# Two transformer blocks: where the feed-forward weights' high and low halves are kept

## What is computed

```python
def conv_ffn(x, ffn_w_in, ffn_conv_w, ffn_conv_b, ffn_w_out):      # first block, both layers
    u, gt = jnp.split(x @ ffn_w_in, 2, axis=-1)
    a = dwconv(gt, ffn_conv_w) + ffn_conv_b
    return (jax.nn.silu(a) * u) @ ffn_w_out

def swiglu(t, w_gate, w_up, w_down):                               # second block
    return (jax.nn.silu(t @ w_gate) * (t @ w_up)) @ w_down
...
        if l % 2 == 0:
            ff = swiglu(h, ffn_w_gate[i], ffn_w_up[i], ffn_w_down[i])
        else:
            ff = moe_swiglu(h, router_w[i], moe_w_gate[i], moe_w_up[i], moe_w_down[i])
```

## Time and profile before

| what | value |
|---|---|
| runs | 2827.49, 2829.64, 2831.5 us; median 2829.64 us |
| profiled execution, span from first to last instruction | 2826.4 us |
| TensorE busy | 2735.9 us (97%) |
| VectorE, ScalarE busy | 2110.1 us (75%), 1694.8 us (60%) |
| DMA | 679.10 MB, mean 240 GB/s |
| the first convolutional layer | 425.17 to 625.43 us |
| the second | 1034.95 to 1237.19 us |
| the gated layer | 1394.49 to 1650.80 us |

### The profile page before, as it was taken

How to read it: one execution, slowest core, us unless ns; L and a number is a source line. 1 busy time by engine, 2 the same in 40 slices (tenths; PEclk the granted TensorE clock), 3 DMA queues, 4 the chain that set the end, 5 groups by cost and what they waited for, 6 DMA issues and landing times.

```text
span 2826.4 us, 42789 instructions
## 1 busy us (share of the span) xinstructions
PE 2735.9 (97%) x18410; PEld 2510.4 (89%) x18418; DVE 2110.1 (75%) x2088; ACT 1694.8 (60%) x1856; POOL 71.6 (3%) x114
## 2 busy tenths in 40 slices
PE   7999999999999999989999999999999999999998
PEld 6999989998999989989899999888888888888886
DVE  5777647876767657777567766688888989888896
ACT  4555446554555546645477753577777767676675
POOL 1000000001000000000010000000000000000000
PEclk9999999999999999999999999999999999999999
DMA  7545447745536467624588732598988989898894
GB/s 235 174 140 168 161 164 254 253 135 154 158 126 200 143 208 249 221 64 150 194 293 291 259 99 90 208 382 334 381 340 337 376 346 371 329 387 340 346 368 183
DMA packets 304404, 679.10 MB, mean 240 GB/s; under 512 B 16560, under 2 KB 238032, under 8 KB 261072
## 3 DMA queue, kind: packets, MB, share of 16 engines
q1 hardware_dynamic: 288832, 617.53, 60.8%
q0 software_dynamic: 15376, 58.75, 6.4%
HBM read 675.19 MB, written 4.69 MB: 241 GB/s over the span
## 4 chain that ended last, share of the span: by engine, by line
PE 74%; DVE 15%; ACT 7%; issue 2%; DMA 1%; SPq 0%; ACTq 0%; DVEq 0%
PE bank L571 71%; DVE w_lo L1366 4%; DVE ew_lo L1875 4%; ACT w_hi L1990 3%; DVE ring_tail L1325 1%; PE bank L1172 1%; ACT ring_tail L2059 1%; DMA ring_head<-in_w_in 1%; DVE ring_tail L1327 1%; PE bank L651 1%; DVE std L1301 1%; PE bank L611 1%; DVE gates L1379 1%; DVE ring_low L1288 0%; PE bank L690 0%
## 5 line engine op out<-in xcount | busy, mean ns | idle before, releaser
L1875 DVE TENSOR_TENSOR ew_lo<-ring_head,ew_hi 128x2048 fp32r<-128x2048 f32 x336 | 759.4, 2288 | 41.4 <-ACT ew_hi L2353 41.4
L2353 ACT CAST ew_hi<-ring_head 128x2048 fp32r<-128x2048 f32 x336 | 640.1, 1914 | 224.5 <-PE bank L571 224.4
L571 PE MATMUL bank<-xs_hi,ring_low 128*128 128x256 f32 (+1 forms) x2608 | 510.9, 283 | 0.0
L571 PEld LDWEIGHTS bank<-xs_hi,ring_low 128*128 128x128 f32 (+1 forms) x2608 | 413.4, 189 | 1.5 <-issue 0.7
L571 PE MATMUL bank<-ew_hi,xe_hi 128*128 128x512 f32 x896 | 353.5, 395 | 0.0
L571 PE MATMUL bank<-ew_hi,xe_lo 128*128 128x512 f32 x896 | 349.4, 390 | 0.0
L571 PE MATMUL bank<-ew_lo,xe_hi 128*128 128x512 f32 x896 | 348.8, 389 | 0.0
L571 PE MATMUL bank<-x_hi,w_hi 128*128 128x256 f32 x1152 | 326.3, 291 | 22.5 <-DVE w_lo L1366 14.7
L1366 DVE TENSOR_TENSOR w_lo<-ring_head,w_hi 128x2048 fp32r<-128x2048 f32 x108 | 247.5, 2292 | 130.5 <-ACT w_hi L1990 130.4
L571 PE MATMUL bank<-x_hi,w_lo 128*128 128x256 f32 x1152 | 319.0, 283 | 0.0
L571 PE MATMUL bank<-x_lo,w_hi 128*128 128x256 f32 x1152 | 318.7, 283 | 0.0
(11 more groups left out here) (425 smaller groups left out, 5483.1 us busy)
## 6 DMA issues: line engine op xcount, KB each, us to landing
ring_head<-in_moe_w_gate SPq DMA_DIRECT2D x112, 1024.0 KB, 7.3
ring_head<-in_moe_w_up SPq DMA_DIRECT2D x112, 1024.0 KB, 7.1
ring_head<-in_moe_w_down SPq DMA_DIRECT2D x112, 1024.0 KB, 7.1
ring_head<-in_w_in SPq DMA_DIRECT2D x82, 1024.0 KB, 5.4
ring_tail<-in_ada_w POOLq DMA_DIRECT2D x48, 1024.0 KB, 7.4
ring_head<-in_ffn_w_in SPq DMA_DIRECT2D x44, 1024.0 KB, 6.1
ring_head<-in_ffn_w_out SPq DMA_DIRECT2D x22, 1024.0 KB, 8.2
ring_head<-in_xa_kv SPq DMA_DIRECT2D x16, 1024.0 KB, 5.4
```

The lines of the kernel that those rows point to most:

```text
L571: ins = nc.tensor.matmul(out, lhsT, rhs, start=start, stop=stop, **kw)
L1875: v.tensor_tensor(ew_lo[:, h, :], ring(c % 6), ew_hi[:, h, :].bitcast(F32), ALU.subtract).then_inc(w_used[c % 6], 1)
L2353: a.copy(ew_hi[:, (e * len(PARTS) + c) % DEPTH_HI, :], ring(c % 6)).then_inc(f.count(part_hi), 1)
```

## The change

The high half gets four buffers in place of two, in the bytes that `w_lo` held. The low half is written in place, into `ring_low[s]`. So the slot is TensorE's until it has gone through the chunk: it gives the slot back (`spent`, the increment of `w_used` rides on the next product), and it counts on `ffn_done` that it has used the high half for the last time, on the product before the chunk's last one. ScalarE waits for `ffn_done` of the chunk four before. Ready chunks are counted over all three layers by `ffn_hi` and `ffn_lo`, in place of one count per buffer or slot. The last chunk's low half goes into a high buffer instead; the next stage writes to that ring slot. The first chunk of a layer has its last two low products behind all others. The silu of the gated layer now waits itself for the gate's bank; ScalarE's product high half waits for the down chunk two steps before; two waits of the next stage count one down further. Apart from that, one load of the second block's mixer takes 32 columns in place of 16.

```diff
-                w_hi, w_lo = (in_scope(ffns, n, 2, CH, dt=F32R) for n in ("w_hi", "w_lo"))
+                w_hi = in_scope(ffns, "w_hi", DEPTH_HI, CH, dt=F32R)
...
-        hi_ready = [sem(f"hi_ready{h}") for h in range(2)]
+        ffn_hi, ffn_lo, ffn_done = sem("ffn_hi"), sem("ffn_lo"), sem("ffn_done")
...
-        cuts = [[(c, CW)] for c in (2064, 2320, 2576)] + [[(1536, 16), (2832, 8)]] + ...
+        cuts = [[(c, CW)] for c in (2064, 2320, 2576)] + [[(1536, 32), (2832, 8)]] + ...
...
+        ffn_base = (0, 3 * (FF1 // CW), 6 * (FF1 // CW))
+        def ffn_slot(i, n):
+            if i == 3 * n - 1:
+                return 3 * ((n - 1) % 2) + 2
+            return (0, 1)[i] if i < 2 else (3, 4, 2, 0, 1, 5)[(i - 2) % 6]
+        def ffn_low(i, n):
+            return w_hi[:, (i + 1) % DEPTH_HI, :] if i == 3 * n - 1 else ring_low[:, ffn_slot(i, n), :]
...
             # TensorE
-                def halves(s, k, n):
-                    h = seq[0] % 2
-                    seq[0] += 1
-                    pe.wait_ge(w_used[s], f.next(w_used[s]))
-                    return [tiles(t[:, h, 0:k * n], k) for t in (w_hi, w_lo)]
+                def halves(k):
+                    i = at[0]
+                    at[0] += 1
+                    pe.wait_ge(ffn_lo, ffn_base[which] + (2 if (which, i) == (2, 0) else i + 1))
+                    return i, tiles(w_hi[:, i % DEPTH_HI, :], k), tiles(ffn_low(i, n), k)
+                def released(out, lhsT, rhs, **kw):
+                    nc.tensor.matmul(out, lhsT, rhs, start=False, stop=False, skip_group_check=True).then_inc(ffn_done, 1)
...
-                                mm(out, hi[:, t, cols], x_lo[:, t, :], False, False)
-                                mm(out, lo[:, t, cols], x_hi[:, t, :], False, t == KD - 1, full if (j, t) == (1, KD - 1) else None)
+                                (released if last else mm)(out, hi[:, t, cols], x_lo[:, t, :], start=False, stop=False)
+                                mm(out, lo[:, t, cols], x_hi[:, t, :], False, t == KD - 1, full if last else None)
+                        spent.append(ffn_slot(i, n))
...
             # VectorE
-            def split_low(s, h, last=None):
-                dve.wait_ge(hi_ready[h], f.next(hi_ready[h]))
-                v.tensor_tensor(w_lo[:, h, :], ring(s), w_hi[:, h, :].bitcast(F32), ALU.subtract).then_inc(w_used[s], 1)
+            def split_low(which, i, n, order=None):
+                dve.wait_ge(ffn_hi, ffn_base[which] + (i if order is None else order) + 1)
+                if i == 3 * n - 1:
+                    dve.wait_ge(ffn_done, ffn_base[which] + i + 2 - DEPTH_HI)
+                v.tensor_tensor(ffn_low(i, n), ring(ffn_slot(i, n)), w_hi[:, i % DEPTH_HI, :].bitcast(F32), ALU.subtract).then_inc(ffn_lo, 1)
...
             # ScalarE
-            def split_high(s, h):
+            def split_high(which, i, n):
+                s = ffn_slot(i, n)
                 eng.wait_ge(ffn_loaded[s], f.next(ffn_loaded[s], 16))
-                a.copy(w_hi[:, h, :], ring(s)).then_inc(f.count(hi_ready[h]), 1)
+                if i >= DEPTH_HI:
+                    eng.wait_ge(ffn_done, ffn_base[which] + i + 1 - DEPTH_HI)
+                a.copy(w_hi[:, i % DEPTH_HI, :], ring(s)).then_inc(ffn_hi, 1)
```

More of the change, by code:

```diff
@@ L369, in due, with ffn_steps @@
             return d * folds // span if 0 < d <= span else folds if d > span else 0
-        def ffn_steps(up, down, n, engine, per, f):
+        ffn_base = (0, 3 * (FF1 // CW), 6 * (FF1 // CW))
+        def ffn_steps(up, down, n):
             up(0, 0)
[L374 to L382, removed]
-            down((n - 1) % 2, n - 1)
@@ L385, in dense_steps @@
-        def dense_steps(split_of, form, finish, n, engine, per, f, side):
-            calls = [0]
[L389 to L418, removed]
+            for i in range(1, n):
+                up(i % 2, i)
+                down((i - 1) % 2, i - 1)
@@ new lines, in ffn_steps, with dense_steps, split @@
+            down((n - 1) % 2, n - 1)
+        def ffn_slot(i, n):
[4 more added lines that the diff above has]
+            return w_hi[:, (i + 1) % DEPTH_HI, :] if i == 3 * n - 1 else ring_low[:, ffn_slot(i, n), :]
+        def dense_steps(split_of, form, finish, n, side):
+            calls = [0]
+            def split():
+                if calls[0] < 3 * n - 2:
+                    split_of(calls[0] + 2)
+                    calls[0] += 1
+                    side(calls[0])
+            for i in range(n):
+                form(i % 2, i)
+                if i < n - 1:
+                    split()
+                finish(i % 2, i)
+                if i < n - 1:
+                    split()
+                split()
@@ L441, in load, with ffn @@
                     at += piece.shape[2] if apart is None else apart
-            def ffn(gate, up_w, down_w, n, per):
+            def ffn(gate, up_w, down_w, n):
                 def up(p, i):
@@ L449, in down @@
                     load(down_w(i), 3 * p + 2, ffn_loaded)
-                ffn_steps(up, down, n, sp, per, f)
+                ffn_steps(up, down, n)
             for l in range(DEPTH):
@@ L738, in down @@
+                                mm(out, lo[:, t, cols], x_hi[:, t, :], False, t == KD - 1, full if last else None)
+                        spent.append(ffn_slot(i, n))
+                def down(p, step):
+                    final = step == n - 1
+                    if final and cover is not None:
                         cover()
-                    hi, lo = halves(3 * p + 2, 2, D)
+                    i, hi, lo = halves(2)
                     pe.wait_ge(act_ready[p], f.next(act_ready[p]))
-                    for t, m in [(t, m) for m in range(KD) for t in range(2)] if last else [(t, m) for t in range(2) for m in range(KD)]:
+                    for t, m in [(t, m) for m in range(KD) for t in range(2)] if final else [(t, m) for t in range(2) for m in range(KD)]:
@@ L748, in down @@
                         else:
-                            mm(out, lo[:, t, cols], act_hi[:, p, t, :], False, False,
-                               down_done if (t, m) == (1, KD - 1) else None, skip_group_check=True)
-                ffn_steps(up, down, n, pe, per, f)
+                            mm(out, lo[:, t, cols], act_hi[:, p, t, :], False, False, down_done if last else None, skip_group_check=True)
+                    spent.append(ffn_slot(i, n))
+                ffn_steps(up, down, n)
             pe.wait_ge(inputs_in, f.next(inputs_in, 64))
@@ L1381, in finish @@
                     v.tensor_tensor(act_lo[:, p, :, :], act[:, p, :, :], act_hi[:, p, :, :].bitcast(F32), ALU.subtract).then_inc(f.count(act_ready[p]), 1)
-                dense_steps(split_low, form, finish, n, dve, per, f, side)
+                dense_steps(lambda i: split_low(which, i, n), form, finish, n, side)
             dve.wait_ge(inputs_in, f.next(inputs_in, 64))
@@ L2060, in scale_part, with dense @@
                 ins.then_inc(mod_scaled, 1)
-            def dense(silu_of, n, per, first, folds):
+            def dense(which, silu_of, n, first, folds):
                 def side(d):
@@ L2067, in side, with finish @@
                         scale_part(first + k)
-                f.bump(gate_full[0])
-                done = {0: gate_full[0], 1: up_full[0], 2: down_done, 3: gate_full[1], 4: up_full[1]}
-                def split(s, h, last):
-                    if last == 5:
-                        eng.wait_ge(down_done, f.now(down_done))
-                    elif (s, last) == (3, 0):
-                        eng.wait_ge(gate_full[0], f.now(gate_full[0]))
-                    else:
-                        eng.wait_ge(done[last], f.next(done[last]))
-                    if s == 5:
-                        f.bump(down_done)
-                    split_high(s, h)
-                def finish(p):
+                downs = f.now(down_done)
+                def finish(p, i):
                     silu_of(p)
                     eng.wait_ge(product_ready[p], f.next(product_ready[p]))
+                    if i >= 2:
+                        eng.wait_ge(down_done, downs + i - 1)
                     a.copy(act_hi[:, p, :, :], act[:, p, :, :]).then_inc(f.count(act_hi_ready[p]), 1)
-                dense_steps(split, lambda p, i: None, finish, n, eng, per, f, side)
+                dense_steps(lambda i: split_high(which, i, n), lambda p, i: None, finish, n, side)
+                f.bump(down_done, n - 1)
             def exps(u):
```

87 lines of the change are left out of this document (46 added, 41 removed), and 10 rows, old and new, of tables (FFN1_TRIP, FFN2_TRIP).

## The result

The changed kernel takes 2804.1 us (median of four runs), the kernel before 2828.56 us beside it: a ratio of 0.991, 95% interval 0.9896 to 0.9925. The forecast was 2812.8 us, in a range from 2806 to 2822 us. Those 1.9 us alone are within the interval, which taken from 2828.56 us reaches from 2799.1 to 2807.3 us; where the forecast went wrong is seen in the trace.

The account below looks back on a forecast made before the run. TensorE, busy nearly all of the span, was taken as the bound, so only its waits or longer work matter. Terms −13.0 − 3.8 = −16.8 us, off the 2829.64 us median, gave 2812.8 us; range 2806 to 2822 us.

Parts of the forecast that it names:

- Waits of the convolutional layers: Two convolutional layers: four high buffers end all TensorE waits for low halves but each layer's very first, −13.0 us.
- the two steps that it puts at 17.4 us: Convolutional layers: two of ten steps, with the fold a place later, have a ScalarE and VectorE loop of 17.4 us.
- The gated layer: Gated layer: the buffer's wait costs 0.32 us a step, so −3.8 us; TensorE still waits 0.44 us a step.
- The loop of 17.7 us: Gated layer: one step's loop through ScalarE and VectorE without the buffer's wait, still more than TensorE's 17.28 us.
- The first rival: All low-half waits go, in the gated layer too: −22.4 us, 2807.2 us; chance 0.09.
- the chunk of 5.76 us: Feed-forward layers: TensorE's time for a chunk of weights, 48 products, one starting every 0.12 us.
- The low half in place: VectorE's subtraction writing into the ring: 0 to 0.2 us less, taken as 0; later slot release also costs 0.
- Release and counts: TensorE's products carry the new increments and none is added: 0, with only 1 us left in the range.
- The refill rival: Loads starting together behind TensorE take longer than 16.9 us, delaying ScalarE's gate rounding: slower, 2858 us; chance 0.06.
- The clock: Layers' last chunks: moved stages may add or remove a lower-clock stretch; 0 in the sum, ±4 us in the range.

Follow-up runs that it names:

- the fastest kernel: Changed kernel with VectorE's fold put behind the product and the activations' low half in the gated layer alone: 2795.0 us, ratio 0.9881.
- another order: VectorE's fold put behind the product: with two high buffers, gated layer alone, 2815.0 us; with four, all three layers 2807.7 us, gated layer alone 2795.0 us.

## Why the prediction was right and wrong

- **Waits of the convolutional layers (−13.0 us): right.** After the first of each layer none over 0.1 us is left. Taking off the shorter products of all chunks but the last (32 x 0.107 = 3.4 us) and, in the second layer, the clock (1.5 us), 6.0 and 6.3 us of the layers' gain remain for the waits; the forecast was 6.5 each. The first wait is 0.19 us, not under 0.1. (The prediction doesn't lay out the two steps that it puts at 17.4 us; the one later wait of the first layer is 0.07 us.)
- **The gated layer (−3.8 us): right.** The loop of 17.7 us came out at 17.72; the layer gained 4.2 us. The first rival, that all waits go, did not come: 12 are left. Its 2807.2 us lies near the result by chance.
- **The step that failed: the chunk of 5.76 us, taken as fixed**, and with it the term *The low half in place*, costed at 0 on VectorE alone. The write is the same, but TensorE reads the low half from another place, and a product's pitch fell from 120.0 to 117.8 ns. In the convolutional layers that is 2 x 3.4 = 6.8 us. In the gated layer the loop binds, so it only made the waits longer: 17.72 − 16.96 = 0.76 us a step in place of the 0.44 forecast. A trace of it stood on the page of before (busy, mean ns): the same kind of product read from the ring, in another stage, is 2 ns shorter there than in the feed-forward layers. The ends of products are modelled in a profile; the pitch of 116.8 ns there, shown above, bears it out.

```profile
L571 PE MATMUL bank<-x_hi,w_lo 128*128 128x256 f32 x1152 | 319.0, 283 | 0.0
...
L571 PE MATMUL bank<-xs_lo,ring_low 128*128 128x256 f32 x958 | 260.2, 281 | 0.0
```

- **The sum with that term:** the forecast −13.0 − 3.8, then −6.8 for the pitch and −1.5 for the clock, is −25.1 us; the three layers became 24.9 us shorter, and 0.9 came back elsewhere. Without the pitch it would have been −18.3 us, 2811.3 us, inside the range.
- **Release and counts (0): right**, by the kernel with two buffers and the low half beside (1.0004).
- **The refill rival (2858 us): did not come.** ScalarE's roundings in the first layer wait 3.1 us for loads in three places, and TensorE waits for none of them.
- **The clock (0, ±4 us): it moved.** In after the second layer's last chunk runs at 1.00 where it had 0.77:

```profile
1209.90:1215.94 6.04, 6.04 (x53) 6.04 (x52) 5.36 (x4) 2.76 (x2) 0.00 (x0) 1.00 0.81 206
```

and in the fastest kernel it has the lower level in part again:

```profile
1207.50:1215.08 7.58, 7.58 (x53) 7.58 (x53) 6.37 (x5) 4.29 (x3) 0.00 (x0) 0.77 0.65 164
```

The Trainium skill's rule on consistent bubbles ("Perfetto Trace Analysis", section "Optimization Strategy": too few buffers, perhaps) held in the convolutional layers, whose waits came back with two buffers and were gone with three. In the gated layer the measurements decide against it: two buffers took 252.7 us and four 252.1, 1.5 us of it for a last chunk at the lower clock that two did not have,

```profile
1618.40:1625.96 7.56, 7.56 (x54) 7.56 (x53) 4.99 (x8) 4.92 (x6) 0.00 (x0) 0.77 0.01 2
```

so two more buffers were worth some 2 us; another order was worth 10.9 us with two buffers and, beside the clock, 8.8 us with four.

## What to carry to other kernels

Before you give a repeating gap more buffers, add up the pitches of the loop through the in-order queues: if the loop is longer than the bottleneck's own work, move an instruction out of it instead, and only in the stage where it is in the way. When an edit changes where an operand lies, ask every engine that reads it, not only the one that writes it; compare the pitch of the same instruction in other stages, to the nanosecond. A gain in the bottleneck's own pitch is worth little while a wait binds (3 us with two buffers), and nearly all of it once the waits are gone.

## What the runs showed of the hardware

A 128x128 weight load and its product with 256 columns start every 120.0 ns at a granted clock of 1.00 when weights and data all lie at bytes 171,424 to 228,768 of the partitions, and every 117.7 to 117.8 ns when the low half lies below 65,664, or x_hi between 82,048 and 90,240. With both it is 117.2 ns in up chunks and 117.8 in gate chunks, and 116.8 ns in the stage that has both halves of the weights in the ring. What it is about the place that counts, a border, a distance or something else, was not tried. The Trainium skill ("SBUF — State Buffer", section "A bandwidth-pool intuition that's wrong (but worth ruling out)") gives TensorE a port for the moving data and a second, independent one for weight loads. No run here shows the ports; the pitch fell by the same 2% whether a weight (the low half) or the moving data (x_hi) was put elsewhere.

The last chunk of a layer comes behind twenty one-column products. In the eleven traces here it falls in part to the lower level of the clock (7.1 us in place of 5.6 from its first weight load to its last) in 15 of the 18 layers in which TensorE waits again and again up to the end, and in 1 of the 15 without such waits. Ending the waits thus seems to bring 1.5 us of clock in a layer besides; why three of the 18 did not fall, and one of the 15 did, is open.
